# Seven block products in place of eight for gate and up, in a two-layer hybrid decoder step

## The reference, cut to what matters

```python
hf = rms_norm(x, p['g_pre_ffn'])                       # 520 tokens x 1024
f = (jax.nn.silu(hf @ p['ffn_gate']) * (hf @ p['ffn_up'])) @ p['ffn_down']
x = x + rms_norm(f, p['g_post_ffn'])                   # D_FF = 2816
```

## Time and profile before

| what | value |
|---|---|
| time, median of 3 runs | 1548.62 us (1546.62 to 1548.86) |
| profiled execution | 1550.66 us, span in the trace 1549.1 us |
| PE busy | 1424.0 us, 11510 matmuls |
| DVE, ACT, POOL busy | 844.8, 537.3, 203.1 us |
| mean granted TensorE clock | 0.96 of full |

### The profile page before, as it was taken

The page is one execution under the profiler, slowest core; times in us unless marked ns, Lnnn a source line. Parts: engine busy times, 40 slices in busy tenths (PEclk is TensorE's granted clock), DMA queues, the critical chain, the costliest instruction groups (busy, mean ns, idle before and its releaser), DMA issues. The chain is left out here.

```text
span 1549.1 us, 28682 instructions
## 1 busy us (share of the span) xinstructions
PE 1424.0 (92%) x11510; PEld 1319.7 (85%) x11510; DVE 844.8 (55%) x1729; ACT 537.3 (35%) x879; POOL 203.1 (13%) x138
## 2 busy tenths in 40 slices
PE   4999878997999999999769998799989999999995
PEld 4889864897999999999657997558979999999994
DVE  5489998735444444222446898976264443442224
ACT  3443234444322222222344422445342232222222
POOL 1334312020000000000040442311200000000010
PEclk8999988999999999999879998999999999999997
DMA  6443231221333332233055333212313233323221
GB/s 222 133 133 96 80 85 44 97 86 44 94 94 95 88 88 83 76 93 93 9 201 146 104 87 88 81 40 87 96 55 95 84 92 95 92 64 94 84 73 55
DMA packets 222718, 141.20 MB, mean 91 GB/s; under 512 B 13514, under 2 KB 218674, under 8 KB 222102
## 3 DMA queue, kind: packets, MB, share of 16 engines
q1 hardware_dynamic: 220006, 132.57, 29.0%
q0 software_dynamic: 2624, 7.48, 1.3%
HBM read 124.66 MB, written 11.77 MB: 88 GB/s over the span
## 5 line engine op out<-in xcount | busy, mean ns | idle before, releaser
L1861 DVE TENSOR_TENSOR w_lo<-ring,w_hi 128x1024 fp32r<-128x1024 f32 (+2 forms) x164 | 179.3, 1093 | 399.2 <-ACT w_hi L1247 399.2
L623 PE MATMUL PS<-u_hi,w_hi 128*128 128x260 f32 x1600 | 325.5, 285 | 15.4 <-DVE u_lo L1982 11.7
L1247 ACT CAST w_hi<-ring 128x1024 fp32r<-128x1024 f32 (+2 forms) x168 | 158.9, 946 | 473.3 <-PE PS L623 473.3
L623 PE MATMUL PS<-u_hi,w_lo 128*128 128x260 f32 x1600 | 322.4, 283 | 0.0
L623 PE MATMUL PS<-u_lo,w_hi 128*128 128x260 f32 x1408 | 283.8, 283 | 0.0
L623 PEld LDWEIGHTS PS<-u_hi,w_hi 128*128 128x128 f32 x1600 | 246.8, 189 | 18.8 <-issue 13.0
L623 PEld LDWEIGHTS PS<-u_hi,w_lo 128*128 128x128 f32 x1600 | 247.4, 189 | 0.0
L623 PEld LDWEIGHTS PS<-u_lo,w_hi 128*128 128x128 f32 x1408 | 218.3, 189 | 0.0
L623 PE MATMUL PS<-hid_hi,w_hi 128*128 128x260 f32 x704 | 141.8, 283 | 3.6 <-ACTq L1404 3.6
L623 PE MATMUL PS<-hid_hi,w_lo 128*128 128x260 f32 x704 | 141.8, 283 | 0.0
L623 PE MATMUL PS<-hid_lo,w_hi 128*128 128x260 f32 x704 | 141.4, 282 | 0.0
(11 more groups left out here) (346 smaller groups left out, 2192.2 us busy)
## 6 DMA issues: line engine op xcount, KB each, us to landing
ring<-in_ffn_gate SPq DMA_DIRECT2D x44, 512.0 KB, 3.7
ring<-in_ffn_up SPq DMA_DIRECT2D x44, 512.0 KB, 3.7
ring<-in_w_in SPq DMA_DIRECT2D x36, 512.0 KB, 3.6
ring<-in_ffn_down SPq DMA_DIRECT2D x32, 384.0 KB, 3.4
ring<-in_ffn_down SPq DMA_DIRECT2D x32, 320.0 KB, 3.0
ring<-in_w_out SPq DMA_DIRECT2D x16, 512.0 KB, 4.1
x_store<-x SPq DMA_DIRECT2D x2, 2080.0 KB, 15.4
x<-x_store SPq DMA_DIRECT2D x2, 2080.0 KB, 7.8
```

The source lines that it names most:

```text
L623: ins = pe.matmul(to[:, h, :], w[:, k - base, :], a[k][:, h * HALF:(h + 1) * HALF], start=(begin and w is whi and a is a_hi), stop=(end an ...
L1247: act.copy(w_hi[part % 2][:, 0:n, :], raw[part % 4][:, 0:n, :]).then_inc(part_hi, 1)
L1861: dve.tensor_tensor(w_lo[part % 2][:, 0:n, :], raw[part % 4][:, 0:n, :], w_hi[part % 2][:, 0:n, :].bitcast(F32), ALU.subtract).then_inc(pa ...
```

## The change

Rounds 0 and 1 (tiles 0 to 3 of gate and of up) stay in the old form. The other nine rounds of a layer (`SEVENS`) each take a pair of gate tiles and a pair of up tiles as a 2 x 2 block matrix: the contraction is halved (4 chunks each), the two tiles are the rows, and the tokens are halved (260 each). Eight block products of 12 matmuls become seven, in Winograd's order of Strassen's form. The right operands (B11, T1, T2, B21, B22, T3, T4) are made once in a layer, from the normalised x. Of the left operands three are blocks of the weights (W11, W12, W22) and four are sums, made by GpSimd for each pair: S1, S3, S2, S4 in this order, S3 in place in the `raw` slot. Every block of 128 x 512 then goes the old way: high part on ACT (`weight_upper`), low part on DVE (`weight_lower`), 12 matmuls on PE (`product`). The accumulated banks are used twice, so ACT copies three of them out (`snap`) and DVE adds them to a later bank (`out_sum`); the last quarter of a pair is used as it lies in PSUM. A half round below is one pair (n = 2r for gate, 2r + 1 for up); the hidden tiles of a round are finished in the gate half of the next one (`gated`, `hidden_upper`, `hidden_lower`). Semaphores are added for this; x is stored to HBM again in the feed-forward part and loaded back for the last sum, since its place holds high parts.

The diff, cut to its core and with less indentation:

```diff
+SUM_BLOCK, HI_BLOCK = [2, 3, 4], [0, 1, 5, 6, 7]
...
+s_made = [over(f"s_made{i}", *block_at(b), [P, KC // 2, P], F32) for i, b in enumerate(SUM_BLOCK)]
+s_lo = [over(f"s_lo{i}", *block_at(b), [P, KC // 2, P]) for i, b in enumerate(SUM_BLOCK)]
+a_hi = [over(f"a_hi{i}", *block_at(b), [P, KC // 2, P]) for i, b in enumerate(HI_BLOCK)]
+raw_lo = [over(f"raw_lo{j}", "ring", j * KC * P, [P, KC, P]) for j in range(4)]
+last_lo = over("last_lo", "ctx_b", 0, [P, KC // 2, P])
...
-DN0 = GU0 + 2 * FFC
+SEVEN_FROM = 2
+SEVENS = FFC // 2 - SEVEN_FROM
+DN0 = GU0 + 4 * SEVEN_FROM
...
-FIRST_FFN = [(q, [k]) for k in range(5) for q in range(3)] + [(0, [5, 6, 7]), (2, [5, 6, 7]), (1, [5, 6, 7])]
+FIRST_FFN = [(q, [k]) for k in range(4) for q in range(3)] + [(0, [4]), (2, [4, 5, 6, 7]), (1, [4]), (0, [5, 6, 7]),
+                                                     (3, []), (1, [5, 6, 7])]
...
+W11, S1, W22, S2, W12, S4, S3 = range(1, 8)
+REUSED = [4, 4, 4, 4, 9, 5, 5, 5, 5, 5, 4, 4, 4, 4]
...
+ACC = [(0, 1, 2), (3, 4, 5)]
...
+def done(r, up, q):
+    return r * 14 + (7 * up + q + 7)
...
-    with sp.Fori(0, FFC // 2) as i:
+    for j in range(4):
+        sp.wait_ge(part_lo, GU0 + j - 3)
+        gate_up(j, (j // 2) * P)
+    sp.wait_ge(x_updated, KC)
+    sp.dma_start(x_store, x_flat).then_inc(x_kept, 16)
+    with sp.Fori(1, SEVEN_FROM + 1) as i:
         for j in range(4):
             sp.wait_ge(part_lo, i * 4 + (GU0 + j - 3))
             gate_up(j, i * (2 * P) + (j // 2) * P)
+    with sp.Fori(1, SEVENS) as r:
+        for up in range(2):
+            for half in range(2):
+                sp.wait_ge(*((weight_lo, r * 14 + (7 * up + W22 - 7)) if half else
+                             (products, r * 14 + (7 * up + W12 - 7))))
+                gate_up(up + 2 * half, r * (2 * P) + (2 * SEVEN_FROM + half) * P)
...
+    for q, up, half in ((0, 0, 0), (2, 0, 1), (1, 1, 0), (3, 1, 1)):
+        sp.wait_ge(*((weight_lo, 14 * SEVENS - 14 + 7 * up + W22 + 7) if half else
+                     (products, 14 * SEVENS - 14 + 7 * up + W12 + 7)))
+        down(q, 0)
+    sp.wait_ge(products, 14 * SEVENS + W22 + 7)
+    sp.dma_start(x_flat, x_store).then_inc(x_back, 16)
+    with sp.Fori(1, KC) as m:
...
+    def product(q, up, to, operand, start):
+        whi, wlo = a_hi[hi_block(q, up if q != W22 else 1 - up)], lo_of(q, up)
+        bhi, blo = b_hi[operand], b_lo[operand]
+        for k in range(KC // 2):
+            for w, b in ((whi, bhi), (whi, blo), (wlo, bhi)):
+                ins = pe.matmul(bank(ACC[up][to])[:, 0:HALF], w[:, k, :], b[:, k, :],
+                                start=(start and k == 0 and w is whi and b is bhi),
+                                stop=(k == KC // 2 - 1 and w is wlo), skip_group_check=True)
+        return ins
+    def seven_products(r, up, first=False, last=False):
+        n3 = r * 6 + 3 * up
+        pe.wait_ge(weight_lo, count(r, up, S2))
+        if first:
+            pe.wait_ge(operand_lo, 3)
+        pe.wait_ge(snapped, n3 + 1)
+        product(S2, up, 0, 2, False).then_inc(products, 1)
+        pe.wait_ge(weight_lo, count(r, up, W12))
+        if first:
+            pe.wait_ge(operand_lo, 4)
+        product(W12, up, 1, 3, True).then_inc(products, 1)
+        pe.wait_ge(weight_lo, count(r, up, S4))
+        if first:
+            pe.wait_ge(operand_lo, 5)
+        pe.wait_ge(snapped, n3 + 2)
+        product(S4, up, 2, 4, False).then_inc(products, 1)
+        pe.wait_ge(weight_lo, count(r, up, S3))
+        if first:
+            pe.wait_ge(operand_lo, 6)
+        pe.wait_ge(snapped, n3 + 3)
+        product(S3, up, 0, 5, False).then_inc(products, 1)
+        if not last:
+            pe.wait_ge(weight_lo, count(r, up, W11 + 7))
+            if up:
+                pe.wait_ge(gate_silu, r * 3 + 3)
+            else:
+                pe.wait_ge(outs_read, r * 7 + 7)
+            product(W11, 1 - up, 0, 0, True).then_inc(products, 1)
+            pe.wait_ge(weight_lo, count(r, up, S1 + 7))
+            product(S1, 1 - up, 2, 1, True).then_inc(products, 1)
+        pe.wait_ge(weight_lo, count(r, up, W22 + 7))
+        if first:
+            pe.wait_ge(operand_lo, 7)
+        pe.wait_ge(outs_read, r * 7 + (7 + (6 if up else 3)))
+        product(W22, up, 0, 6, False).then_inc(products, 3 if last else 1)
...
+    def weight_upper(q, r, up, turn=0):
+        at = up if q != W22 else 1 - up
+        if q in (S1, S2, S3, S4):
+            act.wait_ge(weight_sums, r * 8 + (4 * up + {S1: 1, S3: 2, S2: 3, S4: 4}[q]))
+            source = {S1: s_made[0], S2: s_made[1], S4: s_made[2], S3: raw[up + 2][:, 0:4, :]}[q]
+        else:
+            if q == W11:
+                act.wait_ge(raw_in[up], r * 16 + 16 * (3 + SEVEN_FROM))
+            source = {W11: raw[up][:, 0:4, :], W12: raw[up][:, 4:8, :], W22: raw[up + 2][:, 4:8, :]}[q]
+        act.copy(a_hi[hi_block(q, at)][:, :, :], source if q not in (S1, S2, S4) else source[:, :, :])\
+           .then_inc(weight_hi, turn or 1)
+    def block_free(r, up, q):
+        act.wait_ge(products, r * 14 + (7 * up + q + 7 - REUSED[7 * up + q - 1]))
+    def snap(r, up, which, to, q):
+        act.wait_ge(products, done(r, up, q))
+        act.wait_ge(outs_read, r * 7 + (3 * up + (1, 3, 2)[which]))
+        act.copy(snaps[up][which], bank(ACC[up][to])[:, 0:HALF]).then_inc(snapped, 1)
+    def seven_uppers(r, up, first=False, last=False):
+        before = r if up else r - 1
+        block_free(r, up, S2)
+        weight_upper(S2, r, up)
+        if up:
+            act.wait_ge(outs_read, r * 7 + (7 + 3))
+            act.activation(hid_gate[:, 1, HALF:T], hid_gate[:, 1, HALF:T], ACT.Silu).then_inc(gate_silu, 1)
+        elif not first:
+            hidden_upper(r, 0)
+        snap(r, up, 0, 0, W11)
+        block_free(r, up, W12)
+        weight_upper(W12, r, up)
+        snap(r, up, 1, 2, S1)
+        block_free(r, up, S4)
+        weight_upper(S4, r, up)
+        block_free(r, up, S3)
+        weight_upper(S3, r, up)
+        snap(r, up, 2, 0, S2)
+        if up:
+            act.wait_ge(products, done(r, up, W22))
+            act.activation(hid_gate[:, 1, 0:HALF], bank(ACC[0][0])[:, 0:HALF], ACT.Silu).then_inc(gate_silu, 1)
+        nr = r + 1 if up else r
+        if not last:
+            block_free(nr, 1 - up, W11)
+            weight_upper(W11, nr, 1 - up)
+        if not up and not first:
+            hidden_upper(r, 1)
+        if not last:
+            block_free(nr, 1 - up, S1)
+            weight_upper(S1, nr, 1 - up)
+            block_free(nr, 1 - up, W22)
+        else:
+            act.sem_inc(down_ready, 4)
+            down_upper(0)
+            act.wait_ge(products, 14 * SEVENS + 7 + W22 - REUSED[W22 - 1])
+        weight_upper(W22, r, up, 3 if last else 1)
+        if not up:
+            act.wait_ge(outs_read, r * 7 + (7 + 2))
+            act.activation(hid_gate[:, 0, :], hid_gate[:, 0, :], ACT.Silu).then_inc(gate_silu, 1)
+    def hidden_upper(r, c):
+        at = r * 2 + (2 * SEVEN_FROM + c - 2)
+        act.wait_ge(hidden_made, r * 3 + (2 * SEVEN_FROM + (0, 2)[c] - 2))
+        act.copy(hid_hi[:, bass.ds(at, 1), :], hid_made[:, bass.ds(at, 1), :]).then_inc(hidden_hi, 1)
...
+    def weight_lower(q, r, up, turn=0):
+        at = up if q != W22 else 1 - up
+        f0, f1, f0_lo, f1_lo = raw[up], raw[up + 2], raw_lo[up], raw_lo[up + 2]
+        made, lo = {W11: (f0[:, 0:4, :], f0_lo[:, 0:4, :]), W12: (f0[:, 4:8, :], f0_lo[:, 4:8, :]),
+                    W22: (f1[:, 4:8, :], last_lo[:, :, :]), S3: (f1[:, 0:4, :], f1_lo[:, 0:4, :]),
+                    S1: (s_made[0][:, :, :], s_lo[0][:, :, :]), S2: (s_made[1][:, :, :], s_lo[1][:, :, :]),
+                    S4: (s_made[2][:, :, :], s_lo[2][:, :, :])}[q]
+        dve.wait_ge(weight_hi, count(r, up, q) if q != W22 else count(r, up, q + 7))
+        if q == W11:
+            dve.wait_ge(weight_sums, r * 8 + (4 * up + 3))
+        if q == S2:
+            dve.wait_ge(weight_sums, r * 8 + (4 * up + 4))
+        dve.tensor_tensor(lo, made, a_hi[hi_block(q, at)][:, :, :].bitcast(F32), ALU.subtract).then_inc(weight_lo, turn or 1)
...
+    def out_sum(r, up, which):
+        to, q, s, c, a = ((1, W12, 0, 0, 0), (2, S4, 2, 0, HALF), (0, S3, 1, 1, HALF))[which]
+        dve.wait_ge(products, done(r, up, q))
+        dve.wait_ge(snapped, r * 6 + (3 * up + s + 1))
+        out = hid_made[:, chunk(r, c), a:a + HALF] if up else hid_gate[:, c:c + 1, a:a + HALF]
+        dve.tensor_tensor(out, bank(ACC[up][to])[:, 0:HALF].unsqueeze(1), snaps[up][s].unsqueeze(1), ALU.add)\
+           .then_inc(outs_read, 1)
+    def gated(r, which):
+        dve.wait_ge(gate_silu, r * 3 + (which + 1))
+        if which == 0:
+            dve.wait_ge(outs_read, r * 7 + (7 + 5))
+            h = hid_made[:, chunk(r, 0), :]
+            dve.tensor_tensor(h, h, hid_gate[:, 0:1, :], ALU.mult).then_inc(hidden_made, 1)
+        elif which == 1:
+            dve.wait_ge(outs_read, r * 7 + (7 + 6))
```

(99 more changed lines are left out.)

167 lines of the change are left out of this document (129 added, 38 removed).

## The result

The changed kernel takes 1571.61 us (median of 4 runs, 1571.04 to 1572.64) against 1548.22 for the one before (1546.62 to 1548.86) beside it: ratio 1.0152, 95% interval 1.0139 to 1.0164. The forecast was 1577, slower, range 1525 to 1605. The profiled execution has a span of 1569.8 us, 20.7 more than before, with a granted clock of 0.961 on the mean (0.960 before).

What follows compares the result with a forecast made beforehand. PE bound the old kernel; in new rounds the chain of load, sums and DVE steps would: 16 rounds x 1.84 = +29.4 us, two first rounds -1.3, so +28.1 on 1550.7 is 1578.8, as a median 1577; range 1525 to 1605.

Steps and rivals of the forecast that it cites:

- What bounds, what is saved: Gate and up: PE sets the old round, 23.06 us; 168 matmuls need 20.18, saving 2.88 a round.
- Engines taken alone: Per round of 20.18 us: DVE 12.8, ACT 13.6, GpSimd's eight sums 10.3; each fits taken alone.
- Exclusion: GpSimd sums and DVE operations with two SBUF inputs shut each other out for whole instructions, up to 1.29 us each.
- row of sums: GpSimd's four sums per half round, 5.16 us, lengthened by 0.60 for each of three DVE operations in the gate's half.
- The chain: Load, sums and DVE low parts in series each half round: 13.5 and 11.4 us, together 24.9 a round.
- First rounds: Round 0 of the new form in each layer: 22.4 us, 0.7 under an old round.
- S2's wait: In round 0, S2 waits for the fourth sum, which waits for the first product: about 0.9 us.
- The faster one: Rival: alternation costs less, 1508 us at the chain's floor or about 1545 with half the exclusion left; 25%.
- The clock: PE's gaps of up to 2.3 us would leave it at 2.4 GHz; a falling clock belonged to the 10% upper case.
- x to HBM and back: Store of x (15.4 us) and its load (7.8) both hidden, bound 2 us a layer, taken at 0.
- the signs named: Profile after: POOL about 186 us busier, longer DVE low parts, PE idle 4 to 5 us a round, up's loads about 25 apart.

Runs made afterwards that it cites:

- e1: Changed kernel with the four sums left out (GpSimd only signals, loaded blocks used instead); 1501.6 us, 0.9697 of the kernel before.
- e10: Changed kernel with the sums made on DVE and the two hidden low parts moved to the next round's up half; 1503.8 us, 0.9702 of the kernel before.
- e2: Changed kernel with each sum replaced by two GpSimd memsets that read nothing, loaded blocks used instead; 1501.8 us, 0.9699 of the kernel before.
- e6: Changed kernel with each sum replaced by three GpSimd memsets, loaded blocks used instead; 1546.1 us, 0.9984 of the kernel before.
- e5: Changed kernel using loaded blocks for sums, GpSimd making four same-size subtractions nobody reads in half rounds 1 to 14; 1545.2 us, 0.9984 of the kernel before.
- e4: Changed kernel with W22's high and low part moved ahead of W11's (gate half) or S1's (up half); 1563.6 us, 1.0084 of the kernel before.
- e7: Changed kernel with only half (256 KB) of each second slot loaded; 1561.0 us, 1.0085 of the kernel before.
- e9: Changed kernel with the two hidden low parts moved to the next round's up half, sums still on GpSimd; 1549.7 us, 1.0006 of the kernel before.
- e3: Changed kernel with the same four sums made on DVE instead of GpSimd; 1522.4 us, 0.9823 of the kernel before.

## Why the prediction was right, and where it was off

**What bounds, what is saved.** Right: 168 matmuls alone take 20.09 us in e1 (20.18 forecast), so 3.0 us a round were to be had, and e10 gets 2.8 of them.

**Engines taken alone.** GpSimd's 1.29 us a sum and DVE's 0.69 for 128 x 512 stand in the rows. The Trainium skill, GPSIMD Engine Reference (Elementwise, side-by-side cycle accounting), by which 1.11 us was estimated, is below the rows here too: a sum that meets nothing takes 1.29 to 1.30.

**Exclusion.** The mechanism was right: GpSimd's memsets leave DVE's operations at 0.69 us (e2, e6), and its subtractions, with two SBUF inputs and read by nobody, stretch them to 1.15 to 1.75 and cost 3.3 us a round (e5 over e1). Its place was right too (hidden low part 0, S3, hidden 1 and W11 in the gate half; W11 ahead of the fourth sum in the other). Its size was too large: a DVE operation let in lengthens the row of sums by 1.74 - 1.29 = 0.45 us, not 0.60.

**The chain.** 13.5 and 11.4 us were forecast for the halves; the starts of the first sums are 13.20 and 10.87 apart in the round shown, 13.18 and 11.09 on the mean of all. The 13.20 are the row of sums, 6.62 (500.72 to 507.34; forecast 5.16 + 3 x 0.60 = 6.96), the rest of W11, an output sum, S1, an output sum and W22 to 509.77, 2.43, and 4.15 to the next sum. Of this half the first term is the one mis-sized. In the other half the sums and DVE's steps were right (7.16, forecast 5.16 + 1.80 + 0.33 = 7.29), and from W22 to the next sum it took 3.71 where 3.83 + 0.25 was forecast.

**First rounds and the rest.** 24.27 a round instead of 24.9 is 16 x 0.63 = 10.1 us less than forecast, yet the time is only 5.4 below it (7.4 for the profiled execution, 1571.36 against 1578.8). A first round was forecast 0.7 us under an old one. From the first product (421.33) to the down product's first matmul (642.15) there are 220.8 us, 26.6 more than eight rounds of 24.27; an old round with PE's wait before the down product is 23.06 + 1.78 = 24.84. So a first round costs 1.8 us and gains nothing; the second layer has the same (1191.99 to 1412.72). The step that was mis-sized is S2's wait, 0.9 us in the forecast, 3.47 in the rows:

```profile
426.41 1.45 DVE L2283 TENSOR_TENSOR s_lo<-s_made,a_hi 128x512 fp32r<-128x512 f32 x1 [1.46 <-ACT a_hi L1553]
...
427.91 0.59 PE L1152 MATMUL PS<-b_hi,a_hi 128*128 128x260 f32 x1 [3.47 <-DVE s_lo L2283]
```

The forecast had S2 wait for the fourth sum, which ends at 424.39. Its high part starts only at 425.70, since on ACT the high parts of the last old hidden tile and of two right operands (from 423.25) stand ahead of it, and its low part then takes 1.45 beside a sum. After that wait PE's granted clock, 1.00 until then, is at 0.50 (1.2 GHz) for 3.2 us while PE is busy:

```profile
427.90:431.10 3.20, 3.19 (x14) 3.19 (x15) 3.20 (x4) 0.71 (x2) 0.14 (x1) 0.50 0.00 0
```

Matmuls start 0.22 us apart in it instead of 0.12, some 1.5 us more. e1, without sums, has the same with a wait of 2.53 us. The span's growth of 20.7 us is then 16 x 1.21 = 19.4 in the rounds, 3.5 in the two first rounds and 0.7 in the rounds of the old form, less 3.1 in the rest of the kernel, which was not looked into. That the forecast came so near is in part luck: rounds that were costed too long and first rounds that were costed too short.

**One step of the argument was weaker than its number.** The prediction treated the chain as a sum of lengths: whatever is taken off the load comes off the round. e4 and e7 gave 0.6 and 0.7 us, not all of the 1.6 that e7 took off the load: how long the sums take depends on which DVE operations they meet, and that shifts with the load. e5 says it more strongly: 3.3 of the 4.2 us are there when nobody waits for a sum. Its subtractions start at 499.57, 512.16 and 523.00, halves of 12.59 and 10.84 us against the changed kernel's 13.20 and 10.87, so DVE's longer operations do most of it, and waiting for the sums little. Also DVE was costed by its share of a round, 12.8 us of 20.18; a queue in a fixed order that is full in one half is not helped by room in the other. Moving 1.2 us of it gave 22 us (e9) or 19 (e10 over e3).

**Rivals.** The faster one decided at 23.06 us a round, an exclusion under 2.2 us; e9 gets there by taking two DVE operations out of the row of sums, and its time is that of the kernel before. The clock was expected to hold. In the rounds after the first it did, with gaps up to 1.7 us (1.00 on the mean from 436.3 to 630.5 us); in the first rounds it fell, as said. x to HBM and back was hidden: PE waits for neither in the trace. Of the signs named, POOL's busy time grew by 223 us (186 and more forecast), and DVE's low parts, PE's gaps at S3 and W11 and the 24.3 us between up's loads (515.50 and 539.78) are there.

## What to carry to other kernels

Before work is given to an idle engine, look for two engines' rows over the same time in which one kind of instruction grows and another doesn't; e5 (the same instructions, results unread) prices that effect apart from any dependency. The busy engine may be the better place: here DVE does a sum in 0.60 us of its queue, GpSimd in 1.29, and holds up DVE meanwhile. And add up a queue for each stretch between two waits, not for the round: the same 14 low parts, sums and output sums take 21.39 or 20.26 us a round (e3, e10), by the place of two instructions.

## What the runs showed of the hardware that was not expected

- GpSimd's memset of 128 x 512 float32 takes 0.53 us and leaves DVE's two-input operations at 0.69 (e2), where a subtraction of the same size takes 1.29 and holds them up.
- Between two of GpSimd's sums in a row one DVE operation with two SBUF inputs gets in each time (500 to 508 us of the changed kernel), and costs GpSimd's row 0.45 us, less than its own 0.60 in an undisturbed queue.
- Two engines that start later or earlier against each other change each other's durations, so that a load that lands 0.8 us sooner gave 0.36 us a half round (e7).
- After a wait of 3.47 us (2.53 in e1) the granted clock was at 0.50 in PE's next 3 us; after waits of up to 1.7 us in the later rounds it stayed at 1.00.
